# The gates' projection piece by piece inside the opening of an mLSTM/Conformer inference step

## What is computed

```
hin = rmsnorm(x, g_pre_mix)
z = hin @ w_in                                  # 1024 x 8200
q, k, v, o_gate = heads of z                     # 4 heads of 256 channels
it = z[..., OFF_I:OFF_F] + bif[:M_HEADS]         # the gates: 8 columns of z
lf = log_sigmoid(z[..., OFF_F:OFF_CA] + bif[M_HEADS:])
(C1, n1, m1), hm = mlstm_sequence(carry, (q, k, v, it, lf), n_lead)
...                                              # conv branch, merge by gates, out projection
x = x + rmsnorm(merged @ w_out, g_post_mix)
x = x + rmsnorm(square(relu(rmsnorm(x) @ w_ff1)) @ w_ff2, g_post_ffn)
```

## Time and profile before

| what | value |
|---|---|
| median of 3 runs | 1301.05 us (1300.1 to 1303.42) |
| time of the profiled execution | 1298.64 us |
| its span, first to last instruction | 1296.5 us |
| mean granted TensorE clock | 0.985 of full speed |
| PE busy | 1251.1 us |
| DVE busy | 740.0 us |
| ACT busy | 408.1 us |

### The profile page before, as it was taken

The page is one execution under the profiler, slowest core; times in us unless marked ns, Lnnn a source line. Parts: engine busy times, 40 slices in busy tenths (PEclk is TensorE's granted clock), DMA queues, the critical chain, the costliest instruction groups (busy, mean ns, idle before and its releaser), DMA issues.

```text
span 1296.5 us, 21660 instructions
## 1 busy us (share of the span) xinstructions
PE 1251.1 (96%) x8568; PEld 1218.5 (94%) x8568; DVE 740.0 (57%) x1268; ACT 408.1 (31%) x602; POOL 60.4 (5%) x56
## 2 busy tenths in 40 slices
PE   7999999999999999999999997899999999999996
PEld 7998999999899998999998997799999999999995
DVE  5634579969878987986555423843233334323333
ACT  5442243234124323221463242332132123213432
POOL 2000000000000002000000001830000000000000
PEclk9999999999999999999999998899999999999998
DMA  8343532262334233223222331122222222222212
GB/s 233 97 119 98 145 81 66 83 183 73 92 111 123 78 98 97 75 82 82 65 66 65 117 112 49 34 82 82 78 68 81 67 78 65 80 81 65 66 34 81
DMA packets 192138, 114.49 MB, mean 88 GB/s; under 512 B 13759, under 2 KB 189079, under 8 KB 192066
## 3 DMA queue, kind: packets, MB, share of 16 engines
q1 hardware_dynamic: 170882, 93.53, 25.5%
q10 hardware_dynamic: 21184, 20.02, 4.8%
HBM read 99.32 MB, written 14.21 MB: 88 GB/s over the span
## 4 chain that ended last, share of the span: by engine, by line
PE 86%; DVE 6%; issue 4%; ACT 3%; DMA 1%; DVEq 0%; ACTq 0%; SPq 0%; POOL 0%
PE out L350 76%; PE bank L1419 6%; PE bank L1414 3%; DVE WK L915 2%; DVE CV L915 1%; DVE WK L912 1%; DVE WL L280 1%; DMA WK<-in_x_prompt 1%; PE out L331 1%; ACT CV L531 1%; DVE XL L915 0%; ACT GH L531 0%; ACT WK L531 0%; DVE WK L1081 0%; ACT WH L276 0%
## 5 line engine op out<-in xcount | busy, mean ns | idle before, releaser
L350 PE MATMUL out<-XH,WH 128*128 128x320 f32 (+1 forms) x1664 | 389.5, 315 | 12.2 <-DVE XL L915 9.8
L350 PE MATMUL out<-XH,WL 128*128 128x320 f32 (+1 forms) x1664 | 385.3, 313 | 0.0
L350 PE MATMUL out<-XL,WH 128*128 128x320 f32 (+1 forms) x1664 | 384.3, 312 | 0.0
L350 PEld LDWEIGHTS out<-XH,WH 128*128 128x128 f32 x1664 | 278.7, 189 | 19.5 <-issue 13.7
L350 PEld LDWEIGHTS out<-XH,WL 128*128 128x128 f32 x1664 | 280.4, 189 | 3.3 <-issue 3.1
L350 PEld LDWEIGHTS out<-XL,WH 128*128 128x128 f32 x1664 | 280.6, 189 | 2.9 <-issue 2.7
L280 DVE TENSOR_TENSOR WL<-ST,WH 128x1024 fp32r<-128x1024 f32 x153 | 192.4, 1257 | 121.0 <-ACT WH L276 106.9
L276 ACT ACTIVATE WH<-ST 128x1024 fp32r<-128x1024 f32 x153 | 161.4, 1055 | 224.5 <-PE out L350 183.2
L915 DVE SCALAR_TENSOR_TENSOR CV<-WK,cwu,CV 128x512 f32 (+1 forms) x480 | 226.5, 543 | 0.0
L350 PE MATMUL out<-GH,WH 128*128 128x320 f32 x768 | 176.7, 311 | 6.1 <-DVE WL L280 4.7
L350 PE MATMUL out<-GH,WL 128*128 128x320 f32 x768 | 175.6, 310 | 0.0
(11 more groups left out here) (163 smaller groups left out, 616.2 us busy)
## 6 DMA issues: line engine op xcount, KB each, us to landing
ST<-in_w_in SPq DMA_DIRECT2D x65, 512.0 KB, 4.2
ST<-in_w_ff SPq DMA_DIRECT2D x64, 512.0 KB, 4.1
WK<-in_state_mlstm_C ACTq DMA_DIRECT2D x32, 256.0 KB, 3.7
o_C_sample<-WK ACTq DMA_DIRECT2D x32, 256.0 KB, 2.5
WK<-in_x_prompt SPq DMA_DIRECT2D x8, 512.0 KB, 6.2
ST<-in_w_branch_m SPq DMA_DIRECT2D x8, 512.0 KB, 5.2
ST<-in_w_branch_c SPq DMA_DIRECT2D x8, 512.0 KB, 3.9
ST<-in_w_out SPq DMA_DIRECT2D x8, 512.0 KB, 4.3
```

Of the source, the lines that this page charges most:

```text
L350: last = pe.matmul(out[s][:, h, 0:H], w[:, s, kk, :], x[:, kk, h * H:(h + 1) * H], start=(m < 2), stop=(m >= len(ms) - 2))
```

## The change

The gates' tile is no longer done at once after the last transposes. After the transposes of the third piece PE does the gates' matmuls for the first piece, after the fourth piece's those of the second, and so on (`gates_by_chunk`): 24 matmuls for a piece, with 16 or 128 moving columns, and 48 with 56 or 72 for the piece that crosses the two halves. The constants after the last four pieces are gone. Tile 1 (the first key tile) is done half by half (`half_first`): its first half after the fourth piece's gates, its second after the sixth's. Its place in the first head is taken out. On ACT and DVE the split of tile 1 moves ahead of the last piece's `XH` and `XL`.

```diff
-    def gemm_first(pe, n):
+    def gates_by_chunk(pe, j):
+
+        n = N(0)
+        c_, L = CHUNKS[FIRST[j]]
+        pe.wait_ge(sem("w_lo"), 1)
+        pe.wait_ge(sem("xl"), j + 1)
+        for h in range(2):
+            a_, b_ = max(c_, h * HALF), min(c_ + L, (h + 1) * HALF)
+            if a_ >= b_:
+                continue
+            for kk in range(KT):
+                for i, (w, x) in enumerate(((WH, XH), (WL, XH), (WH, XL))):
+                    last = pe.matmul(out[0][:, h, a_ - h * HALF:b_ - h * HALF], w[:, 0, kk, :], x[:, kk, a_:b_],
+                                     start=(i == kk == 0), stop=(i == 2 and kk == KT - 1))
+        if j == 5:
+            last.then_inc(sem("tile_done"), 1)
+
+    def half_first(pe, n, h, ready):
 
         s, H = n.par % 2, half(n)
...
+        for i, (w, x) in enumerate(((WH, XH), (WL, XH), (WH, XL))):
+            pe.wait_ge(sem(("xh", "xh", "xl")[i]), ready)
+            pe.wait_ge(sem(("w_hi", "w_lo", "w_lo")[i]), val(n) + 1)
...
-            for j in range(3, 6):
+            for j in range(3, 5):
                 x_hi(j)
             hi(N(1))
+            x_hi(5)
...
-            for j in range(3, 6):
+            for j in range(3, 5):
                 x_lo(j)
             lo(N(1))
+            x_lo(5)
...
-                wait(pe, "xl", j - 2)
+                wait(pe, "xl", (0, 0, 0, 1, 2, 4)[j])
                 for kk in range(KT):
                     tr(x_psum(j)[:, kk, :], xtok0[0:CHUNKS[c][1], c, kk * P:kk * P + P],
                        "t_x" if kk == KT - 1 else None)
-                keep_busy(4)
-            gemm_first(pe, N(0))
+                if j >= 2:
+                    gates_by_chunk(pe, j - 2)
+                else:
+                    keep_busy(4)
+            half_first(pe, N(N_HEADS0), 0, 4)
+            gates_by_chunk(pe, 4)
+            gates_by_chunk(pe, 5)
+            half_first(pe, N(N_HEADS0), 1, 6)
...
-                    if r < 8:
+                    if r == 0 and first:
+                        pass
+                    elif r < 8:
                         gemm(pe, n + r, XH, XL)
```

More of the change, by code:

```diff
@@ L314, in x_psum @@
         L = CHUNKS[FIRST[j]][1]
-        t = (PB[0], PB[1], out[1])[j % 3]
+        t = (PB[0], PB[1], out[1], PB[0], PB[1], PB[0])[j]
         return t[:, :, :].rearrange("p h (k t) -> p (h k) t", t=P)[:, :, 0:L]
-    def gemm_first(pe, n):
-        s, H = n.par % 2, half(n)
[L321 to L333, removed]
+    def gates_by_chunk(pe, j):
[14 more added lines that the diff above has]
+    def half_first(pe, n, h, ready):
+        s, H = n.par % 2, half(n)
+        for i, (w, x) in enumerate(((WH, XH), (WL, XH), (WH, XL))):
+            pe.wait_ge(sem(("xh", "xh", "xl")[i]), ready)
+            pe.wait_ge(sem(("w_hi", "w_lo", "w_lo")[i]), val(n) + 1)
+            for kk in range(KT):
+                last = pe.matmul(out[s][:, h, 0:H], w[:, s, kk, :], x[:, kk, h * H:(h + 1) * H],
+                                 start=(i == kk == 0), stop=(i == 2 and kk == KT - 1))
+        if h:
+            last.then_inc(sem("tile_done"), 1)
     def gemm(pe, n, xh, xl, gaps=(), rhs_ready=None):
```

## The result

The changed kernel takes 1339.78 us in the median (1338.63 to 1346.58, 4 runs) against 1300.84 for the kernel before, timed beside it (1300.1 to 1303.42, 4 runs): a ratio of 1.0314, 95% interval 1.0296 to 1.0332, some 39 us or 3% slower. Its profiled execution took 1340.81 us with a span of 1338.6, 42.1 more than the span before. The side was forecast, the size was not: on the base of the forecast, 1301.05 us, the ratio gives 1341.9, beyond the range of 1319 to 1340.

The account below looks back on a forecast made before the run. PE, busy 96% of the span, was taken as the bound. At full clock 20.1 later less 0.6 regained gave +19.5; a clock returning at 34 made it +26, so 1301.05 + 26 = 1327 us, range 1319 to 1340.

Parts of the forecast that it names:

- PE in front of WL: In the opening, PE has no work from 13.88 to about 20.55, waiting for WL of tile 0.
- 168 small matmuls at the load's price: Gates by piece: 168 matmuls at 0.107 us each at full clock, 0.214 at half; 18.0 us in place of 7.25.
- The row with one column: Profile row of float32 passes with one moving column and the same weight load, 0.102 us a step; decides for the load.
- a price by the columns' stream: Rival for the gates' small matmuls: 8.8 us in all, net +10.3, 1311; chance 0.05.
- The clock: In the opening, PE meets the gates' pieces at half clock after its idle; how much slow work depends on its return.
- The middle case: Clock returns at the fifth piece's transposes (34), tile 1's second half ends at 55.2; net +26, chance 0.40.
- then the rest at full clock: In the opening, after the clock's return at 34.2, the remaining pieces and tile 1's halves run at full clock to 55.2.
- the late case: Rival: clock returns only in tile 1's dense first half, its second half ends at 65.9; +37, 1338 to 1340; chance 0.25.
- So of the 7.2 us only 0.6 come back: Behind the cache, tile 1's 7.2 us lead is lost to waits of 3.6 and 2.9 us before tiles 2 and 3.
- my step on the clock: Behind the parameter transposes the clock may fall again; tile 2 may lose 1.7 us, hidden by tile 3's wait (2.9).
- D: Delay of everything behind the parameter transposes: 20.1 us at full clock, 26.7 with the clock back at 34.
- Behind that the kernel is as before, and the shift stays to the end: After the opening and the first tiles nothing changes in length, so the opening's shift stays unchanged to the end.

Follow-up runs that it names:

- e5_tile1_only: Kernel before with only tile 1 moved, in two halves, ahead of the parameter transposes, gates in one go: 1306.75 us, ratio 1.0044.
- e1_after_pad: Changed kernel with 140 waits on a long-raised semaphore (70 instructions) in PE's idle before the first piece's gates: 1330.78 us, ratio 1.0242.
- e2_before_pad: Kernel before with 256 waits on a raised semaphore (128 instructions) ahead of everything: 1322.08 us, ratio 1.015.
- e10_constants_out: Kernel before without the constants behind the last four pieces, nothing in their place, 64 instructions shorter: 1310.83 us, ratio 1.0108.

## Why the forecast was right and wrong

**PE in front of WL: right.** PE stood 6.63 us from 13.9, released by WL, and the fourth piece's transposes came at 25.8.

**168 small matmuls at the load's price: right.** The steps are 0.111 and 0.213 us, for 16, 56, 72 and 128 columns alike, where I had 0.107 and 0.214. The row with one column was the right one to read, and a price by the columns' stream (8.8 us for all of them) would have been wrong by a factor of two.

**The clock: right in kind, the term mis-sized by 4.4 us.** The middle case has the second half of tile 1 end at 55.2; it ended at 59.7. The third piece ended 0.8 later than counted (the clock returned at 35.5, not 34), and the second fall cost 1.4 in the fourth piece (6.49 against 5.1), 2.0 in tile 1's first half (5.62 against 3.6) and 0.2 behind it. My step "then the rest at full clock" failed. Its ground was half right: in the idle the clock did fall, as forecast (0.85 in the mean of 13.9 to 20.5, 0.50 from 20.5). But the idle is not the only thing that loses it: with the idle filled it fell at the end of the 16-column piece, and it stayed up where that piece was replaced. The row that stood against the late case, transposes and pauses at 1.00, did not hold either: in the changed kernel the last of the same transposes ran at 0.50 (the mean of 64 to 68). What the engine did before each fall of the opening is thus known; why the clock returned at 29, at 35.5 or only at 54 in kernels with nearly the same pieces stays open. That is also where the spread of these kernels' times comes from, as far as their profiles tell.

**"So of the 7.2 us only 0.6 come back": right in kind, 0.0 in size.** The waits before tiles 2 and 3 were there, 3.4 and 0.7 us; the second is short because tile 2 ran in part at half clock, which my step on the clock had foreseen and hidden in it. And `e5_tile1_only` shows the mechanism alone. The cache's first transposes ran at a fallen clock (the eight take 1.87 us against 1.21 in the trace before), so tile 3's WL came 0.5 later than D says.

**"Behind that the kernel is as before, and the shift stays to the end": wrong, 11 us.** This is the step that failed. It put the cost behind the opening at nothing; the runs show 10.2 us at two jumps back in its place and 0.9 elsewhere. It took the code behind the change as unchanged because its text and its data are. Its place in PE's program, and with it the number of blocks that the loop touches, is not, and `e1_after_pad` (the change without the stalls), `e2_before_pad` (the stalls without the change) and `e10_constants_out` show it from three sides. Without the stalls, in `e1_after_pad`, the change costs 30.0 us in the medians, 1330.78 against 1300.74, which is inside the range.

Summed in the profiled execution: 26 forecast, 4.4 for the clock, 0.6 for the lead, 11.1 at and behind the jumps, 42.1. Had the clock taken the late case, +37, the opening alone would have looked like the result; the trace shows that it was another sum.

## What to carry to other kernels

Cutting a projection into pieces of few columns multiplies the weight loads, here 168 for 48, and from 16 to 128 columns each matmul took the same 0.11 us. In the opening, matmuls of 16, 56 or 72 columns went ahead of every fall of the clock but those at pauses. Work moved ahead of a wait gives nothing if it was what covered that wait (`e5_tile1_only`, 7.3 us moved and 7.3 lost). And whoever adds or removes instructions ahead of a loop should look at the jumps back and at the instruction queue's packets first: 43 or 44 against 61 or 62 told the two kinds of kernel apart here at a glance, and padding is the test that separates such a loss from the change itself.

## What the runs showed of the hardware that I had not expected

- A jump back whose loop lies badly makes PE stand 3.2 to 3.7 us in the head loop, and costs 3.8 to 5.7 us with the half clock behind it (eight jumps in four kernels). In the feed-forward loop it is 2.6 and 2.4 us of standing, 3.2 and 2.9 in all (two jumps in one kernel). A shift of 64 instructions was enough to bring it about, and two such jumps bring 18 packets on the instruction queue, where a loop that lies well brings none.
- A wait on a semaphore that is already raised takes PE 54 ns, so it is no free filler.
- The clock can fall without any pause: 1.00 to 0.50 in the middle of unbroken small matmuls, with PE busy 4.00 of 4 us.
